# Attention's turned probabilities leave PSUM by two engines instead of one

## The chip, the cores and the metric

One core of one Trainium2 chip. The core has TensorE (PE, matmuls; its weight loads are shown as PEld), VectorE (DVE), ScalarE (ACT), GpSimd (POOL) and SyncE (SP), each with its own program, which it works through in order. They keep step by semaphores. The metric is the device time of one execution in microseconds (us), as the median over runs.

## The reference

Two decoder layers over 512 positions of width 1024: a gated short convolution, then dilated window attention, each followed by a mixture of experts. The change lies in the attention of the second layer: 3 groups of 16 heads with 64 columns each. For one group:

```python
scores = jnp.einsum("bnqrhd,bnkrhd->bnrhqk", qs, kb) * (Dh ** -0.5)
scores = jnp.where(mask[None, :, None, None], scores, -jnp.inf)
m = jnp.max(scores, axis=-1, keepdims=True)
p = jnp.exp(scores - m)
denom = jnp.sum(p, axis=-1)
o = jnp.einsum("bnrhqk,bnkrhd->bnqrhd", p, vb.astype(jnp.float32))
```

Each group's output is divided by its denominator, and the groups are merged with weights from m and denom; then comes the output projection.

## The kernel before

The kernel runs the 16 head slots in two stages (s = 0, 1) of 8. A stage first projects q, k and v for its 8 slots in three groups, then calls `attend(s)`, which every engine has in its own version. `attend` goes through 16 units. A unit u is a pair of heads (head block hb = u // 4, heads hd = 0 and 1) and one tile of 128 queries (t = u % 4). Its keys are up to four tiles of 128: two of the near group and one each of the two far groups, so 512 columns, or 384 where t = 0 and there is no tile before the first.

One unit passes through these steps:

- `scores(u)` on TensorE: q times k into PSUM bank 2*(u%2)+hd. Signal `scored`.
- `mask_scores(u)` on VectorE (L1375): mask, and the row's extreme value, into `prob[u%2]` in SBUF. Four instructions, two per head. Signal `masked`.
- `softmax_exp(u)` on ScalarE (L844): four exponentials in place, with the sums. Signal `expd`.
- `turn_probs(u)` on TensorE (L1764): transposes of the probabilities, head 0 into PSUM bank 4, head 1 into bank 5. Signal `p_turned`, one per head.
- `probs_back(u)` on VectorE (L1387): both banks are copied to `probT[u%2]` in SBUF. Signal `pt_ready`, one per head.
- `weighted(u)` on TensorE (L1778): v times probT into banks 6 and 7. Signal `pv_done`.

The order is written out by hand. In a round u TensorE does scores(u+1), weighted(u-1), turn_probs(u); VectorE mask_scores(u+1), probs_back(u); ScalarE softmax_exp(u+1). At u = 4, 8 and 12 ScalarE also runs `store_heads` (L854, L857), which waits for weighted(u-1) and copies banks 6 and 7 to near_o and far_o; weighted(u) of a new block waits for it (`o_stored`). In stage two ScalarE also has `heads_hi` (L862) at u = 2 and 6, and VectorE `heads_lo` at u = 4 and 8.

Behind the 16 units VectorE does `scales(s)`: 16 small copies (L1394), then a short chain to stat_exp (L1398, signal `gap_in`), which ScalarE takes up (L878), and head_scale (L1404). ScalarE casts a weight block before that (`hi(U_QKV + 7)`). TensorE goes on with matmuls of the next projection (L314 to L316) and, between them, `spread_scales` (L1732), which needs head_scale: in stage one much later, in stage two after 12 matmuls.

Of the kernel before, what the change touches and what calls it, by code (L numbers as in the profile page):

```python
# [31 lines left out]
P = 128  # L32
# [25 lines left out]
def build(nc, x, positions, norm_mix, norm_ffn, norm_final, conv_w_in, conv_w, conv_w_out, attn_w_qkv,  # L58
# [19 lines left out]
    with ExitStack() as ctx:  # L78
# [180 lines left out]
        def sem(name):  # L259
# [26 lines left out]
        scored, masked, expd, p_turned, pt_ready, pv_done, o_stored = (  # L286
            sem("scored"), sem("masked"), sem("expd"), sem("p_turned"), sem("pt_ready"),
            sem("pv_done"), sem("o_stored"))
# [368 lines left out]
        def _(act):  # L657
# [177 lines left out]
            def softmax_exp(u, s):  # L835

                t, buf = u % NT, prob[u % 2]
                for hd in range(2):
                    head = 2 * (u // NT) + hd
                    for far in range(2):  # L840
# [4 lines left out]
                                       scale=-1.0, accum_out=st[:, 1, head:head + 1]).then_inc(expd, 1)  # L845

            def store_heads(hb, s):

                act.wait_ge(pv_done, s * 16 + 4 * hb + 4)
                if s + hb == 0:  # L850
                    act.wait_ge(h_saved, 16 * NT)
                if hb == 0 and s == 1:
                    act.wait_ge(merged, 4)
                act.activation(near_o[s][:, hb, :].rearrange("p (r b a) -> p b r a", r=NT, b=NT),  # L854
                               ps[:, 6, :].rearrange("p (b r a) -> p b r a", r=NT, b=NT), ACT.Copy
                               ).then_inc(o_stored, 1)
                act.activation(far_o[s][:, hb, :], ps[:, 7, :], ACT.Copy).then_inc(o_stored, 1)  # L857
# [7 lines left out]
            def attend(s):  # L865
# [3 lines left out]
                for u in range(16):  # L869
                    if u + 1 < 16:  # L870
                        softmax_exp(u + 1, s)
                    if u % NT == 0 and u:
                        store_heads(u // NT - 1, s)
                    if s == 1 and u in (2, 6):
                        heads_hi(u // 4)
# [50 lines left out]
        def _(dve):  # L926
# [453 lines left out]
            def probs_back(u, s):  # L1380

                if u >= 2:
                    dve.wait_ge(pv_done, s * 16 + u - 1)
                for hd in range(2):
                    dve.wait_ge(p_turned, s * 32 + 2 * u + hd + 1)
                    k0 = P if u % NT == 0 else 0
                    dve.tensor_copy(probT[u % 2][:, hd, k0:S], ps[:, 4 + hd, k0:S]).then_inc(pt_ready, 1)  # L1387

# [91 lines left out]
        def _(pe):  # L1480
# [276 lines left out]
            def turn_probs(u, s):  # L1757

                for hd in range(2):
                    pe.wait_ge(expd, s * 64 + 4 * u + 2 * hd + 2)  # L1760
                    if u >= 1:
                        pe.wait_ge(pt_ready, s * 32 + 2 * (u - 1) + hd + 1)
                    for n in range(1 if u % NT == 0 else 0, 4):
# [4 lines left out]
            def weighted(u, s):  # L1768

                hb, t = u // NT, u % NT  # L1770
                if t == 0 and hb:
                    pe.wait_ge(o_stored, s * 8 + 2 * hb)
                pe.wait_ge(pt_ready, s * 32 + 2 * u + 2)
                keys = ([(0, 0, t - 1)] if t else []) + [(1, 0, t), (2, 1, t), (3, 2, t)]
# [106 lines left out]
```

## Time and profile before

| | |
|---|---|
| Median of 3 runs | 1459.32 us (1459.04 to 1459.7) |
| Profiled execution, its own time | 1458.0 us |
| Its span, first to last instruction | 1456.3 us |
| Busy: TensorE, VectorE, ScalarE | 1363.7, 990.7, 782.9 us |
| Mean granted clock of TensorE | 0.976 |
| Attention, stage one | 737.4 to 789.3 us |
| Attention, stage two | 1003.3 to 1055.2 us |

The profile is of one execution. In a timeline row the first number is the start in us from the span's start and the second the length; one row can hold several instructions (the count stands behind x), and then the length runs from the first start to the last end. Square brackets hold the time the engine sat idle before, and who ended it. An instruction can start before the one ahead of it has ended, so the distance between two starts is often less than the length.

### The profile page before, as it was taken

Reading aid. Unit: us, or ns where it says so; the run is one execution under the profiler, and the core shown is the slowest. Engines: PE = TensorE matmul, PEld = TensorE weight load, DVE = VectorE, ACT = ScalarE, POOL = GpSimd, SP = SyncE. Lnnn points to the kernel's source line nnn. Section 1 sums busy time; section 2 is a strip of 40 time slices with the busy share of each in tenths; the row PEclk is TensorE's granted clock in tenths of the full one; section 3 lists DMA queues with packets and bytes.
Section 4 is the critical chain, followed back from the end, with each engine's and each line's share of the span. In section 5 each row is a group of like instructions: output and inputs, shape, how many; then the busy total and the mean of one; then the engine's idle time right before and its main releaser. Section 6 shows DMA issues by size and latency. Waiting matters only on the chain.

```text
span 1456.3 us, 21039 instructions
## 1 busy us (share of the span) xinstructions
PE 1363.7 (94%) x7335; PEld 1128.7 (78%) x7335; DVE 990.7 (68%) x1289; ACT 782.9 (54%) x947; POOL 209.3 (14%) x309
## 2 busy tenths in 40 slices
PE   4999987999999999999998999999888699999995
PEld 4888776888888877888877888887767588888884
DVE  6455367999999986243466535254846799898998
ACT  4221244888878843523365252335714478888883
POOL 4000021111111212021100202020002111111121
PEclk9999997999999999999999999999999699999998
DMA  6228416999999954232200213221032699999994
GB/s 220 87 95 317 180 72 218 368 391 387 393 391 391 352 226 145 91 111 88 87 31 30 87 59 116 87 87 59 2 116 119 225 368 390 395 379 391 390 356 174
DMA packets 85108, 308.43 MB, mean 212 GB/s; under 512 B 12034, under 2 KB 12058, under 8 KB 68661
## 3 DMA queue, kind: packets, MB, share of 16 engines
q1 hardware_dynamic: 76404, 291.73, 54.0%
q0 software_dynamic: 8640, 15.86, 2.9%
q8 instruction: 39, 0.64, 0.2%
q14 instruction: 25, 0.20, 0.0%
HBM read 291.72 MB, written 31.46 MB: 222 GB/s over the span
## 4 chain that ended last, share of the span: by engine, by line
PE 86%; DVE 7%; issue 2%; ACT 2%; DMA 1%; SPq 1%; POOLq 0%; DVEq 0%; POOL 0%; ACTq 0%
PE ps L314 26%; PE ps L316 25%; PE ps L315 25%; PE ps L1778 2%; PE ps L1591 1%; DVE probT L1387 1%; PE ps L1849 1%; PE ps L1732 1%; PE ps L1764 1%; DVE h L1206 1%; DMA x_rows<-hn_rows,tok_list 1%; ACT prob L844 1%; ACT W_hi L720 1%; PE ps L1606 1%; PE ps L1615 1%
## 5 line engine op out<-in xcount | busy, mean ns | idle before, releaser
L314 PE MATMUL ps<-W_hi,xT_hi_all 128*128 128x512 f32 x1408 | 559.8, 398 | 7.7 <-DVE xT_lo_all L1420 4.5
L316 PE MATMUL ps<-W_hi,xT_lo_all 128*128 128x512 f32 x1408 | 551.8, 392 | 0.0
L315 PE MATMUL ps<-W_lo,xT_hi_all 128*128 128x512 f32 x1408 | 550.4, 391 | 0.0
L1135 DVE TENSOR_TENSOR W_lo<-m_raw,W_hi 128x2048 fp32r<-128x2048 f32 x192 | 435.9, 2291 | 58.7 <-ACT W_hi L720 58.7
L720 ACT ACTIVATE W_hi<-m_raw 128x2048 fp32r<-128x2048 f32 x192 | 367.3, 1915 | 48.2 <-PE ps L316 47.6
L314 PEld LDWEIGHTS ps<-W_hi,xT_hi_all 128*128 128x128 f32 x1408 | 265.7, 189 | 66.1 <-issue 5.0
L316 PEld LDWEIGHTS ps<-W_hi,xT_lo_all 128*128 128x128 f32 x1408 | 265.6, 189 | 57.7
L315 PEld LDWEIGHTS ps<-W_lo,xT_hi_all 128*128 128x128 f32 x1408 | 266.0, 189 | 51.9
L940 DVE SCALAR_TENSOR_TENSOR W_lo<-raw,mix_gain,W_hi 128x512 fp32r<-128x512 f32 x144 | 99.7, 754 | 183.1 <-ACT W_hi L664 183.1
L664 ACT ACTIVATE W_hi<-raw,mix_gain 128x512 fp32r<-128x512 f32 x144 | 92.2, 712 | 228.4 <-issue 224.8
L630 POOL TENSOR_TENSOR qk_rot<-rope_a,rope_b 128x512 f32<-128x512 f32 x48 | 62.3, 1302 | 375.6 <-DVE rope_b L1449 375.6
L946 DVE TENSOR_TENSOR W_lo<-raw,W_hi 128x2048 fp32r<-128x2048 f32 x20 | 45.9, 2293 | 89.1 <-ACT W_hi L668 88.9
L668 ACT ACTIVATE W_hi<-raw 128x2048 fp32r<-128x2048 f32 x20 | 38.2, 1911 | 107.1 <-PE ps L316 104.9
L314 PE MATMUL ps<-xT_hi_all,W_hi 128*128 128x512 f32 x192 | 75.7, 394 | 0.0
L315 PE MATMUL ps<-xT_lo_all,W_hi 128*128 128x512 f32 x192 | 75.2, 392 | 0.0
L316 PE MATMUL ps<-xT_hi_all,W_lo 128*128 128x512 f32 x192 | 75.2, 392 | 0.0
L509 POOL TENSOR_SCALAR msq<-ssq 128x1 f32<-128x1 f32 x20 | 8.9, 444 | 377.7 <-ACT square_out L674 377.6
L737 ACT ACTIVATE xT_hi_all<-ps 128x1024 fp32r<-128x1024 f32 x32 | 32.9, 1027 | 55.8 <-PE ps L1591 55.8
L1446 DVE TENSOR_TENSOR rope_a<-ps,cos_t 128x512 f32<-128x512 f32 x48 | 33.1, 689 | 25.9 <-POOL qk_rot L630 14.1
L1387 DVE COPY probT<-ps 128x512 f32<-128x512 f32 (+1 forms) x64 | 39.1, 653 | 12.4 <-PE ps L1764 11.7
L674 ACT ACTIVATE square_out<-h 128x1024 f32<-128x1024 f32 x20 | 21.1, 1057 | 48.3 <-DVE h L956 30.0
L600 POOL COPY dest_col<-dest_list 128x1 int32 x28 | 18.2, 651 | 181.5 <-ACT y_rows_sb L758 181.5
(232 smaller groups left out, 1458.3 us busy)
## 6 DMA issues: line engine op xcount, KB each, us to landing
m_raw<-in_w_gate_dram SPq DMA_DIRECT2D x64, 1024.0 KB, 7.7
m_raw<-in_w_up_dram SPq DMA_DIRECT2D x64, 1024.0 KB, 8.6
m_raw<-in_w_down_dram SPq DMA_DIRECT2D x64, 1024.0 KB, 8.7
raw<-in_attn_w_qkv_dram SPq DMA_DIRECT2D x36, 1024.0 KB, 5.1
raw<-in_conv_w_in_dram SPq DMA_DIRECT2D x12, 1024.0 KB, 5.1
y_rows<-zero_rows SPq DMA_DIRECT2D x2, 4096.0 KB, 17.4
y_pick<-y_rows SPq DMA_DIRECT2D x16, 512.0 KB, 7.3
raw<-in_conv_w_out_dram SPq DMA_DIRECT2D x4, 1024.0 KB, 5.8
```

Source lines behind the costliest of these rows:

```text
L314: pe.matmul(o, a_hi, b_hi, start=first, stop=False)
L315: pe.matmul(o, a_hi, b_lo, start=False, stop=False)
L316: return pe.matmul(o, a_lo, b_hi, start=False, stop=last)
L630: pool.tensor_tensor(qk_rot[:, r, :], rope_a[r % 2][:, :], rope_b[r % 2][:, :], ALU.add).then_inc(rope_added, 1)
L664: ins = act.activation(W_hi[uc % SPLIT][:, k, :], raw[uc % RAW][:, k, :], ACT.Copy, scale=mix_gain[:, 4 * (uc % 2) + k:4 * (uc % 2) + k + 1])
L668: act.activation(W_hi[uc % SPLIT][:, :, :], raw[uc % RAW][:, :, :], ACT.Copy).then_inc(split_hi, 1)
L720: act.activation(MW_hi[c % MSPLIT][:, :, :], m_raw[c % MRAW][:, :, :], ACT.Copy).then_inc(s["hi"], 1)
L940: ins = dve.scalar_tensor_tensor(out=W_lo[uc % SPLIT][:, k, :], in0=raw[uc % RAW][:, k, :], scalar=mix_gain[:, 4 * (uc % 2) + k:4 * (uc % ...
L946: dve.tensor_tensor(W_lo[uc % SPLIT][:, :, :], raw[uc % RAW][:, :, :], W_hi[uc % SPLIT][:, :, :].bitcast(F), ALU.subtract).then_inc(split_ ...
L1135: dve.tensor_tensor(MW_lo[c % MSPLIT][:, :, :], m_raw[c % MRAW][:, :, :], MW_hi[c % MSPLIT][:, :, :].bitcast(F), ALU.subtract).then_inc(s[ ...
L1387: dve.tensor_copy(probT[u % 2][:, hd, k0:S], ps[:, 4 + hd, k0:S]).then_inc(pt_ready, 1)
L1446: dve.tensor_tensor(av, t, cb, ALU.mult)
```

## The change

In `probs_back` VectorE keeps only the copy of head 0. ScalarE gets a new function `second_back(u, s)`, which copies head 1 from bank 5 with an ACTIVATE Copy of the same size. It stands in ScalarE's round u behind softmax_exp(u+1) and, at u = 4, 8, 12, behind store_heads. The semaphore `pt_ready` becomes two, one for each head; weighted(u) waits for both.

```diff
@@ -284,7 +284,7 @@
         rope_in, rope_added, qk_turned, qkT_ready, v_ready = (
             sem("rope_in"), sem("rope_added"), sem("qk_turned"), sem("qkT_ready"), sem("v_ready"))
         scored, masked, expd, p_turned, pt_ready, pv_done, o_stored = (
-            sem("scored"), sem("masked"), sem("expd"), sem("p_turned"), sem("pt_ready"),
+            sem("scored"), sem("masked"), sem("expd"), sem("p_turned"), [sem("pt_ready0"), sem("pt_ready1")],
             sem("pv_done"), sem("o_stored"))
         gap_in, gap_out, scales_ready, spread, merged = (
             sem("gap_in"), sem("gap_out"), sem("scales_ready"), sem("spread"), sem("merged"))
@@ -844,6 +844,14 @@
                         act.activation(buf[:, hd, cols], buf[:, hd, cols], ACT.Exp, bias=st[:, 0, head:head + 1],
                                        scale=-1.0, accum_out=st[:, 1, head:head + 1]).then_inc(expd, 1)
 
+            def second_back(u, s):
+
+                if u >= 2:
+                    act.wait_ge(pv_done, s * 16 + u - 1)
+                act.wait_ge(p_turned, s * 32 + 2 * u + 2)
+                k0 = P if u % NT == 0 else 0
+                act.activation(probT[u % 2][:, 1, k0:S], ps[:, 5, k0:S], ACT.Copy).then_inc(pt_ready[1], 1)
+
             def store_heads(hb, s):
 
                 act.wait_ge(pv_done, s * 16 + 4 * hb + 4)
@@ -871,6 +879,7 @@
                         softmax_exp(u + 1, s)
                     if u % NT == 0 and u:
                         store_heads(u // NT - 1, s)
+                    second_back(u, s)
                     if s == 1 and u in (2, 6):
                         heads_hi(u // 4)
                 hi(U_QKV + 7, s * 3 + 2)
@@ -1381,10 +1390,9 @@
 
                 if u >= 2:
                     dve.wait_ge(pv_done, s * 16 + u - 1)
-                for hd in range(2):
-                    dve.wait_ge(p_turned, s * 32 + 2 * u + hd + 1)
-                    k0 = P if u % NT == 0 else 0
-                    dve.tensor_copy(probT[u % 2][:, hd, k0:S], ps[:, 4 + hd, k0:S]).then_inc(pt_ready, 1)
+                dve.wait_ge(p_turned, s * 32 + 2 * u + 1)
+                k0 = P if u % NT == 0 else 0
+                dve.tensor_copy(probT[u % 2][:, 0, k0:S], ps[:, 4, k0:S]).then_inc(pt_ready[0], 1)
 
             def scales(s):
 
@@ -1759,7 +1767,7 @@
                 for hd in range(2):
                     pe.wait_ge(expd, s * 64 + 4 * u + 2 * hd + 2)
                     if u >= 1:
-                        pe.wait_ge(pt_ready, s * 32 + 2 * (u - 1) + hd + 1)
+                        pe.wait_ge(pt_ready[hd], s * 16 + u)
                     for n in range(1 if u % NT == 0 else 0, 4):
                         ins = pe.transpose(ps_r[:, 4 + hd, n * P:(n + 1) * P],
                                            prob_r[u % 2][:, hd, n * P:(n + 1) * P], ident_r[:, :])
@@ -1770,7 +1778,8 @@
                 hb, t = u // NT, u % NT
                 if t == 0 and hb:
                     pe.wait_ge(o_stored, s * 8 + 2 * hb)
-                pe.wait_ge(pt_ready, s * 32 + 2 * u + 2)
+                pe.wait_ge(pt_ready[0], s * 16 + u + 1)
+                pe.wait_ge(pt_ready[1], s * 16 + u + 1)
                 keys = ([(0, 0, t - 1)] if t else []) + [(1, 0, t), (2, 1, t), (3, 2, t)]
                 for n, g, kt in keys:
                     for hd in range(2):
```

The program of ScalarE in stage one, from the last exponentials of softmax_exp(5) (buffer prob_101) over the store of the first head block. Before:

```order
L844 ACTIVATE prob_101,near_stat<-prob_101,near_stat 128x256 [waits masked]
L844 ACTIVATE prob_101,stat<-prob_101,stat 128x256 [waits masked]
L844 ACTIVATE prob_101,near_stat<-prob_101,near_stat 128x256 [waits masked]
L844 ACTIVATE prob_101,stat<-prob_101,stat 128x256 [waits masked]
L854 ACTIVATE near_o_106<-ps 128x4x4x32 [waits h_saved,pv_done]
L857 ACTIVATE far_o_108<-ps 128x512
L844 ACTIVATE prob_100,near_stat<-prob_100,near_stat 128x256 [waits masked]
```

After, the same place; probT_104 is the buffer of the even units:

```order
L844 ACTIVATE prob_101,near_stat<-prob_101,near_stat 128x256 [waits masked]
L844 ACTIVATE prob_101,stat<-prob_101,stat 128x256 [waits masked]
L844 ACTIVATE prob_101,near_stat<-prob_101,near_stat 128x256 [waits masked]
L844 ACTIVATE prob_101,stat<-prob_101,stat 128x256 [waits masked]
L862 ACTIVATE near_o_106<-ps 128x4x4x32 [waits h_saved,pv_done]
L865 ACTIVATE far_o_108<-ps 128x512
L853 ACTIVATE probT_104<-ps 128x384 [waits p_turned,pv_done]
L844 ACTIVATE prob_100,near_stat<-prob_100,near_stat 128x256 [waits masked]
```

The copy of u = 4 stands behind exp(5) and the two stores, ahead of exp(6); before, exp(6) followed the stores. In the same way each of the 16 units of a stage has its copy behind the four exponentials of the next unit.

The end of ScalarE's program in stage one, after: the last exponential of u = 15, then the copies of u = 14 and 15, the weight cast, and what answers VectorE's scales.

```order
L844 ACTIVATE prob_101,stat<-prob_101,stat 128x256 [waits masked]
L853 ACTIVATE probT_104<-ps 128x512 [waits p_turned,pv_done]
L853 ACTIVATE probT_105<-ps 128x512 [waits p_turned,pv_done]
L664 ACTIVATE W_hi_53<-raw_58,mix_gain 128x512 [waits mix_gain_in,unit_done,raw_in2]
L664 ACTIVATE W_hi_53<-raw_58,mix_gain 128x512 x3
L887 ACTIVATE stat_exp<-stat_exp 128x64 [waits gap_in]
```

The two copies have come in ahead of the weight cast, which stood right behind the exponentials. On TensorE no matmul moves; the first one of weighted(u) has one wait more. Before, at u = 0:

```order
L1778 MATMUL ps<-probT_104,v_all 64x128 [waits pt_ready]
L1778 MATMUL ps<-probT_104,v_all 64x128 x5
```

After:

```order
L1787 MATMUL ps<-probT_104,v_all 64x128 [waits pt_ready1,pt_ready0]
L1787 MATMUL ps<-probT_104,v_all 64x128 x5
```

The wait on `pt_ready` has become one on `pt_ready1` and one on `pt_ready0`.

## Rows read from the trace of the kernel before

**Rows 1.** The page: its head, and busy time by engine.
```profile
span 1456.3 us, 21039 instructions
...
PE 1363.7 (94%) x7335; PEld 1128.7 (78%) x7335; DVE 990.7 (68%) x1289; ACT 782.9 (54%) x947; POOL 209.3 (14%) x309
```

**Rows 2.** Busy time by stretch, the two attention stages; PEclk is the granted clock.
```profile
737.40:789.30 51.90, 45.30 (x552) 37.88 (x553) 42.40 (x167) 37.28 (x138) 0.00 (x0) 1.00 0.01 2
1003.30:1055.20 51.90, 45.30 (x552) 37.88 (x552) 44.30 (x169) 38.52 (x137) 0.00 (x0) 1.00 0.01 2
```

**Rows 3.** Who waited for whom in stage one: total, times, longest.
```profile
ACT prob L844 <- DVE near_stat L1375: 12.5, 11, 1.6
...
PE ps L1778 <- DVE probT L1387: 2.9, 5, 1.1
...
PE ps L1778 <- ACT far_o L857: 2.2, 3, 0.7
```

**Rows 4.** ScalarE: two source lines (ns min/median/max), two forms in stage one.
```profile
L857 ACT ACTIVATE far_o<-ps x8: 575/577/593, 754.1 to 1058.0; 128x512 f32<-128x512 f32 x8
...
L907 ACT ACTIVATE v_all<-ps,rstd x16: 687/689/698, 660.7 to 1002.6; 128x512 f32<-128x512 f32 x16
...
L844 ACT ACTIVATE prob<-prob,stat 128x256 f32<-128x256 f32 x32 | 15.8, 494 | 0.0
...
L844 ACT ACTIVATE prob<-prob,near_stat 128x128 f32<-128x128 f32 x8 | 3.2, 395 | 3.5 <-DVE near_stat L1375 3.5
```

**Rows 5.** Timeline of stage one, u = 4: start, length, line.
```profile
754.08 0.57 ACT L857 ACTIVATE far_o<-ps 128x512 f32<-128x512 f32 x1
754.55 0.50 ACT L844 ACTIVATE prob<-prob,near_stat 128x256 f32<-128x256 f32 x1
...
754.71 0.88 PE L1778 MATMUL ps<-probT,v_all 128*64 128x128 f32 x12 [0.74 <-ACT far_o L857]
```

**Rows 6.** Timeline of stage one, u = 0.
```profile
742.18 0.49 ACT L844 ACTIVATE prob<-prob,stat 128x256 f32<-128x256 f32 x1
...
742.31 0.88 PE L1778 MATMUL ps<-probT,v_all 128*64 128x128 f32 x12
```

**Rows 7.** Timeline of stage one, u = 2 and 3.
```profile
747.07 0.49 ACT L844 ACTIVATE prob<-prob,stat 128x256 f32<-128x256 f32 x1
...
748.14 1.09 PE L1778 MATMUL ps<-probT,v_all 128*64 128x128 f32 x16 [0.23 <-DVE probT L1387]
749.17 0.87 PE L1764 MATMUL ps<-ident_r,prob_r 128*128 128x128 f32 x8
749.97 0.70 PE L1749 MATMUL ps<-qkT 64*128 64x256 f32 x4
...
751.16 1.09 PE L1778 MATMUL ps<-probT,v_all 128*64 128x128 f32 x16
```

**Rows 8.** Timeline of stage one, the end.
```profile
784.71 2.55 ACT L664 ACTIVATE W_hi<-raw,mix_gain 128x512 fp32r<-128x512 f32 x4
...
786.93 1.29 DVE L1387 COPY probT<-ps 128x512 f32<-128x512 f32 x2 [1.72 <-PE ps L1764]
...
785.26 1.09 PE L1778 MATMUL ps<-probT,v_all 128*64 128x128 f32 x16 [1.11 <-DVE probT L1387]
786.29 0.87 PE L1764 MATMUL ps<-ident_r,prob_r 128*128 128x128 f32 x8
788.28 1.09 PE L1778 MATMUL ps<-probT,v_all 128*64 128x128 f32 x16 [1.11 <-DVE probT L1387]
```

**Rows 9.** Timeline of stage two, heads_hi at u = 2.
```profile
1013.42 1.04 ACT L862 ACTIVATE xT_hi_all<-near_o 128x1024 fp32r<-128x1024 f32 x1
...
1017.02 1.09 PE L1778 MATMUL ps<-probT,v_all 128*64 128x128 f32 x16
```

**Rows 10.** Timeline behind stage two, the first spread matmuls.
```profile
1058.85 1.97 PE L1732 MATMUL ps<-ident,head_scale 128*64 128x128 f32 x32 [0.62 <-DVE head_scale L1404]
```

**Rows 11.** Timeline behind stage one, VectorE's scales.
```profile
791.24 0.23 DVE L1398 TENSOR_TENSOR stat_exp<-stat_min,stat 128x64 f32<-128x64 f32 x1
```

## The prediction

> **What bounds the kernel now.** I read the page first: TensorE is busy for 1363.7 of 1456.3 us [rows 1], so only a stretch where it waits can give anything back. The change touches one piece of code, the attention loop, which runs twice: 737.4 to 789.3 us and 1003.3 to 1055.2 us. The table of these two windows shows the same 51.9 us and the same 45.30 us of TensorE work in both, at full granted clock and with DMA idle [rows 2]. So 6.6 us per stage is all that is on offer, 13.2 us in the two. What follows each stage on TensorE is the projection's matmuls, whose operands are there, so that an end which moves moves everything after it by the same amount.
>
> The waits of the first stage say who ends those 6.6 us [rows 3]. 2.9 us in 5 waits are for VectorE's copy of the turned probabilities (probT, L1387): these the change could touch. 2.2 us in 3 waits are for ScalarE's store of the finished heads (far_o, L857). The remaining 1.5 us lies mostly in the opening, before the first exponentials are done. ScalarE waits 12.5 us for the row minima, so it looks as if it had room for 16 copies. When it has that room is the whole question, since it takes its work in program order.
>
> **The order of one unit.** TensorE does scores(u+1), weighted(u-1), turn(u). ScalarE did softmax_exp(u+1), four exponentials, and at u = 4, 8, 12 then the two copies of store_heads. The new copy for unit u stands behind all of these. weighted(u) needs it, and comes on TensorE right behind scores(u+2). A copy that must queue behind exponentials of the next unit is late; one that finds them done is not. I go through the five kinds of place by rows.
>
> **Price of one copy on ScalarE.** No row of before shows it. The nearest is far_o L857: PSUM to SBUF, 128x512, 577 ns, and the next instruction starts 0.47 to 0.48 us after it [rows 4, 5]. The dear end is L907, the same shape with a per-partition scale, 689 ns; the cheap end is an exponential half as wide, 494 ns [rows 4]. I take 0.58 us, since the new copy, like far_o, has no scale pointer. Going from 128 to 256 columns costs an exponential 0.10 us [rows 4], so the 384-wide copy of a block's first unit is 0.48 us, and its follower starts 0.38 us after it. From the end of a copy to TensorE's start I take 0.05 us: far_o 754.08 + 0.57 = 754.65, matmul 754.71 [rows 5].
>
> **1. Opening, u = 0.** ScalarE has exp(0) and exp(1) back to back, the last at 742.18, 0.49 us long, so the copy starts at 742.67, ends at 743.15, and weighted(0) starts at 743.20. Before it started at 742.31, straight behind the scores [rows 6]. Cost +0.89 us. VectorE's copy of this head had been done by then; on ScalarE it stands behind four exponentials that nobody wants yet.
>
> **2. Turn of a head block, u = 4, 8, 12.** far_o starts at 754.08 and the next instruction at 754.55. That slot now takes the copy: 754.55 + 0.48 + 0.05 = 755.08, against 754.71 [rows 5]. The wait for far_o is followed by one for the copy. Cost +0.37 us, three times: +1.11.
>
> **3. Third unit of a block, u = 2, 6, 10.** The last exponential of exp(3) starts at 747.07, so the copy runs 747.56 to 748.14 and TensorE starts at 748.19; now it starts at 748.14, after a wait of 0.23 for VectorE [rows 7]. One wait takes the place of the other: +0.05, three times, +0.15.
>
> **4. u = 14.** exp(15) holds ScalarE until 784.71; 784.71 + 0.58 + 0.05 = 785.34 against 785.26 [rows 8]. +0.08.
>
> **5. u = 15.** Here ScalarE has nothing before the copy, and the two copies run side by side. turn(15) starts at 786.29, VectorE's first copy at 786.93, 0.64 later, after half the transposes. The other half takes 0.40 more, since eight transposes take 0.80, from 749.17 to the scores at 749.97 [rows 7]. So the copy starts at 787.33 and weighted(15) at 787.96 against 788.28 [rows 8]. -0.32.
>
> The other units cost nothing. At u = 3, turn(3) starts at 749.17, its second half is turned 0.64 + 0.40 later at 750.21, and the four exponentials ahead of the copy are two short and two long ones, done by about then; the copy is in by 750.84, and weighted(3) started at 751.16 [rows 7]. So it has 0.3 us in hand, and u = 5 has as much, where TensorE and ScalarE have both been set back by the block's turn. In the second stage heads_hi (L862, 1.04 us) stands behind the copy at u = 2 and 6. From 1013.42 on: copy 0.48, heads 0.95, four exponentials 1.76, then the copy of u = 3 with 0.63 ends at 1017.24, while weighted(3) started at 1017.02 [rows 9]. These 0.22 us are hidden: scores(5) is already issued, so exp(5) and the store behind it come when they came, and weighted(4) waits longer than that in any case.
>
> **Sum.** Stage one: 0.89 + 1.11 + 0.15 + 0.08 - 0.32 = +1.91. Stage two has the same terms, but its end hangs on VectorE: the spread matmuls wait 0.62 us for head_scale [rows 10], whose chain starts as soon as VectorE's copies end. With one copy fewer it starts 1.29 - 0.69 = 0.60 earlier, and TensorE's own path 0.32 earlier with 0.62 of slack, so the end term is -0.60: +1.63. Together +3.54 us. ScalarE's part of the head_scale chain stays covered: it must be free when VectorE hands over, 791.24 + 0.23 - 0.60 = 790.9, and after the copy (787.33 + 0.48) and the four weight casts (2.55) it is free at 790.4 [rows 8, 11]. If that cover failed, the cost would be some tenths in stage two only. The weight casts themselves start 3 us later, but VectorE's half of that split stands behind head_scale in its program, so no DMA is released later for it; DMA is idle in both stages [rows 2]. The two semaphores instead of one add a second wait to weighted(u); o_stored beside pt_ready was already such a pair at u = 4, and nothing there shows a price. VectorE's saved time, 16 x 0.6 us a stage, buys nothing while its masks start on scores.
>
> The profiled execution took 1458.0 us, so it would be 1461.5. The median of the runs shown is 1459.32, 1.3 above it, and the times are compared with that: 1459.32 + 3.54 = **1462.9 us**, 0.24% slower. About 0.2% (2.9 us) is what a measurement of this kernel can tell from no change, so this stands close to that line.
>
> **Bounds.** Nine of the copies in a stage lie on the path in this account (1 + 3 + 3 + 1 + 1). With 0.49 us a copy it is 9 x 0.09 = 0.8 less in each stage, total +1.9. With 0.69 it is 9 x 0.11 = 1.0 more in each, total +5.5.
>
> **Rivals.**
> - **Faster: the copies run side by side everywhere.** For it: ScalarE's 12.5 us of waiting and VectorE with both copies in a row [rows 3, 8]. Then the three waits of 0.23 vanish and both closing waits shrink by 0.32, the opening and far_o stay as they are: -1.3 in stage one, -1.6 in stage two, 1456.4 us. It decides if ScalarE reaches the copy before TensorE has turned the second head. Against it: at 742.67, 747.56, 754.55 and 784.71 ScalarE comes free only after that, and its idle time lies ahead of the exponentials, not behind them. The Trainium skill speaks for this rival: "Perfetto Trace Analysis", section Optimizing Scalar/DVE Operations, says that where VectorE is saturated, handing work to ScalarE may make sense, and "TensorEngine Tiling (Array Packing)", section PSUM Bottleneck, says to use both engines to empty PSUM. By that rule the copies' waits would fall; this trace agrees only at u = 15, and there by 0.32 us. Chance 6%.
> - **No change that can be measured: the copy is nearer the cheap end**, or a place hides some tenths. TensorE would start weighted(4) at 754.99 instead of 755.08, and so on; +1.9, 1461.2 us. Against it: far_o is the same operation on the same engine. Chance 28%.
> - **Slower by more: the copy is as dear as L907**, or waiting for the fresh transposes costs ScalarE more than it cost VectorE: +5.5, 1464.8 us. Against it: L907 has the scale pointer. Chance 10%.
>
> My forecast has 56%, with its own range from 1462.2 to 1464. Slower by over 0.2% is forecast plus the dear copy, 66%; within 0.2% is 28%; faster by over 0.2% is 6%. For the 8 in 10 I go from 1460.4, a little under the cheap copy, to 1465.1, over the dear one; the faster rival stays outside.
>
> **What would show it.** In the profile after: 32 ScalarE copies of about 580 ns and 480 ns; no idle time of ScalarE ahead of those at u = 0, 2, 4, 14; TensorE's waits before the weighted matmuls naming ScalarE's probT, about 1.1 us at u = 4, 8, 12 in place of 0.74, about 0.9 at u = 0, 0.28 at u = 2, 0.8 at u = 15; each stage 53.8 us. The wait for head_scale after stage two is near 0.3 us. It is wrong if weighted(4) starts no later behind far_o, if weighted(0) follows the scores at once, or if a copy lasts outside 0.49 to 0.69 us. It is also wrong if a later stretch, the projection or the experts, changes its length by more than 0.5 us.

## The result and the profile after

The changed kernel took 1463.22 us (median of 8 runs, 1460.83 to 1464.43), the kernel before beside it 1459.26 us (8 runs, 1458.24 to 1460.8). The ratio, run against run, is 1.0024 with a 95% interval of 1.0013 to 1.0035, which is 1.9 to 5.1 us: slower, and by no more than what can just be told. The forecast was 1462.9 us. A second comparison, further down, gave 1.0031 [1.0019, 1.0042].

The page after, for [rows 1], its head and busy time by engine:

```profile
span 1460.2 us, 21093 instructions
...
PE 1361.8 (93%) x7335; PEld 1128.4 (77%) x7335; DVE 973.1 (67%) x1257; ACT 798.1 (55%) x979; POOL 209.0 (14%) x309
```

VectorE has lost 17.6 us of work and 32 instructions, ScalarE has gained 15.2 us and 32, and the span is 3.9 us longer. Taking work off VectorE has bought nothing. The windows of the two stages, for [rows 2] (a window here is longer because the stages are):

```profile
737.70:792.30 54.60, 44.90 (x553) 38.15 (x553) 34.06 (x153) 43.89 (x153) 0.00 (x0) 1.00 0.01 2
1006.30:1060.90 54.60, 45.07 (x553) 38.23 (x553) 36.19 (x155) 45.36 (x153) 0.00 (x0) 1.00 0.01 2
```

TensorE does the same work at the same granted clock, over a longer time: the loss is waiting. Who waits for whom in stage one, for [rows 3] (total us, times, longest):

```profile
DVE prob L1384 <- PE ps L1760: 17.6, 15, 8.8
...
PE ps L1787 <- ACT probT L853: 8.6, 9, 1.4
ACT prob L844 <- DVE near_stat L1384: 7.8, 8, 1.6
```

The five waits for VectorE's probT and the three for far_o (2.9 and 2.2 us) are gone. Nine waits for ScalarE's probT stand in their place, 8.6 us. Exactly the nine places of the prediction: u = 0, 2, 4, 6, 8, 10, 12, 14 and 15. ScalarE's waiting for VectorE's minima fell from 12.5 to 7.8 us, so it did have room, but the room lay ahead of its exponentials. VectorE's saved time turned into waiting: 7.8 us more for scores in this stage (17.6 for 9.8) and 3.5 us more for transposes (10.0 for 6.5).

To see where the time goes I use three marks that every kernel has: stage one and stage two, each from its first score matmul to the start of weighted(15), and for stage two also the first matmul of the spread.

| profile | stage one | stage two | stage two to spread | spread to end of span |
|---|---|---|---|---|
| before | 50.80 | 50.83 | 55.50 | 397.4 |
| changed | 53.53 | 53.49 | 57.84 | 396.1 |
| changed, run again | 53.52 | 53.53 | 57.87 | 396.5 |
| before, run again | 50.81 | 50.83 | 55.50 | 397.2 |

In these two pairs a stage repeats to 0.05 us. The rest of the span does not: the code behind the spread is the same in all kernels here and took 395.9 to 397.4 us in 13 profiles, and stage one started anywhere from 737.2 to 739.8 us. Between the two stages all show 215.1 us. So the change costs 2.73 us in stage one and 2.34 us up to the spread, 5.07 us, where the prediction had 1.91 and 1.63. In the first pair of profiles the unchanged code behind the spread gave 1.4 us of it back. Where it did so can be read from the granted clock, here over 14 us from 16 us behind the first spread matmul on, before and then after:

```profile
1074.80:1088.80 14.00, 9.47 (x41) 7.45 (x36) 5.50 (x5) 2.86 (x2) 0.00 (x0) 0.76 0.56 195
1080.20:1094.20 14.00, 9.47 (x43) 7.57 (x38) 5.49 (x5) 2.86 (x2) 0.00 (x0) 0.88 0.54 200
```

TensorE had the lower of its two clocks (1.2 and 2.4 GHz) for a larger part of this stretch before (0.76) than after (0.88), and at its end the kernel before was 0.9 of the 1.4 us behind. All 13 profiles fall into two groups by the clock of this stretch: seven with 0.76 took 396.9 to 397.4 us behind the spread, six with 0.88 took 395.9 to 396.7.

The timeline after. The opening, for [rows 6] (start, length, engine, line; in brackets the wait and whom for):

```profile
742.43 0.49 ACT L844 ACTIVATE prob<-prob,stat 128x256 f32<-128x256 f32 x1
...
742.92 0.47 ACT L853 ACTIVATE probT<-ps 128x384 f32<-128x384 f32 x1
...
743.53 0.88 PE L1787 MATMUL ps<-probT,v_all 128*64 128x128 f32 x12 [0.91 <-ACT probT L853]
```

The copy starts when the last exponential of the next unit is through, with no idle time ahead of it. At u = 2 and 3, for [rows 7]:

```profile
748.78 0.57 ACT L853 ACTIVATE probT<-ps 128x512 f32<-128x512 f32 x1
...
749.50 1.09 PE L1787 MATMUL ps<-probT,v_all 128*64 128x128 f32 x16 [0.50 <-ACT probT L853]
...
751.33 0.70 PE L1757 MATMUL ps<-qkT 64*128 64x256 f32 x4
...
752.40 1.09 PE L1787 MATMUL ps<-probT,v_all 128*64 128x128 f32 x16
```

At u = 4, for [rows 5]; the copy has taken the slot behind far_o:

```profile
755.43 0.58 ACT L865 ACTIVATE far_o<-ps 128x512 f32<-128x512 f32 x1
755.91 0.47 ACT L853 ACTIVATE probT<-ps 128x384 f32<-128x384 f32 x1
...
756.53 0.88 PE L1787 MATMUL ps<-probT,v_all 128*64 128x128 f32 x12 [1.32 <-ACT probT L853]
```

The end, for [rows 8]:

```profile
787.79 0.57 ACT L853 ACTIVATE probT<-ps 128x512 f32<-128x512 f32 x1
790.51 0.60 ACT L853 ACTIVATE probT<-ps 128x512 f32<-128x512 f32 x1 [2.15 <-PE ps L1772]
...
788.51 1.09 PE L1787 MATMUL ps<-probT,v_all 128*64 128x128 f32 x16 [1.36 <-ACT probT L853]
...
791.25 1.09 PE L1787 MATMUL ps<-probT,v_all 128*64 128x128 f32 x16 [0.84 <-ACT probT L853]
```

Only at u = 15 does ScalarE wait for the transposes rather than TensorE for ScalarE's queue, and only there is the wait shorter than before (0.84 against 1.11). One number returns in every row: from the end of the copy to the matmul it is not 0.05 us. 742.92 + 0.47 = 743.39, and TensorE starts at 743.53; 755.91 + 0.47 = 756.38 and 756.53; 787.79 + 0.57 = 788.36 and 788.51. It is 0.14 to 0.15 us each time.

### The profile page after: what moved, and what is told of

Read it like the earlier page. It is cut to its first block, busy times and chain, and to the rows that moved or that the text cites. A ratio compares the mean times of both kernels' runs of the same rounds, so it can differ in the third digit from the quotient of the medians.

```text
span 1460.2 us, 21093 instructions
## 1 busy us (share of the span) xinstructions
PE 1361.8 (93%) x7335; PEld 1128.4 (77%) x7335; DVE 973.1 (67%) x1257; ACT 798.1 (55%) x979; POOL 209.0 (14%) x309
## 4 chain that ended last, share of the span: by engine, by line
PE 85%; DVE 5%; ACT 5%; issue 2%; DMA 1%; SPq 1%; POOLq 0%; DVEq 0%; ACTq 0%; POOL 0%
PE ps L314 26%; PE ps L316 25%; PE ps L315 25%; ACT prob L844 2%; PE ps L1599 1%; PE ps L1787 1%; PE ps L1858 1%; PE ps L1740 1%; PE ps L1772 1%; DVE h L1215 1%; DMA x_rows<-hn_rows,tok_list 1%; ACT W_hi L720 1%; PE ps L1757 1%; PE ps L1614 1%; PE ps L1502 1%
## 5 line engine op out<-in xcount | busy, mean ns | idle before, releaser
L1787 PE MATMUL ps<-probT,v_all 128*64 128x128 f32 x480 | 33.3, 278 | 17.0 <-ACT probT L853 17.0
L1384 DVE CUSTOM_DVE_ANT_0 prob<-ps,near_mask 128x256 f32<-128x256 f32 (+1 forms) x64 | 24.8, 388 | 34.9 <-PE ps L1760 34.9
```

The source lines that it names most:

```text
L1787: ins = pe.matmul(ps[HD * hd:HD * hd + HD, 6 if g == 0 else 7, t * P:(t + 1) * P], v_all[:, g, kt, head * HD:head * HD + HD], probT[u % 2] ...
```

## Experiments

Two questions. Is it the place in ScalarE's program that costs, or what the copies cost anywhere? And whose are the 0.09 us that each release is longer: ScalarE's as the engine that copies, or the second semaphore's? Differences of time are against the kernel before run on the same chip.

**One semaphore** (changed kernel, both copies increment one counter):

```
-  ...ps[:, 5, k0:S], ACT.Copy).then_inc(pt_ready[1], 1)      # ScalarE; VectorE alike
+  ...ps[:, 5, k0:S], ACT.Copy).then_inc(pt_ready, 1)
-  pe.wait_ge(pt_ready[0], s * 16 + u + 1)
-  pe.wait_ge(pt_ready[1], s * 16 + u + 1)
+  pe.wait_ge(pt_ready, s * 32 + 2 * u + 2)
   ...in turn_probs, which now waits for both copies and not for its head's alone
-  pe.wait_ge(pt_ready[hd], s * 16 + u)
+  pe.wait_ge(pt_ready, s * 32 + 2 * u)
```

> The changed kernel with one semaphore pt_ready again, which both engines raise; ScalarE still copies the second head. Measured so far from the first score matmul to the start of weighted(15): before 50.80 and 50.83 us in the two stages, changed 53.53 and 53.49. In the changed trace TensorE starts 0.15 us after the end of ScalarE's copy (copy of u = 14 787.79 + 0.57 = 788.36, matmul 788.51), where I had taken 0.05. Theory A (the second wait on weighted costs 0.10 us each time the copy is what it waits for): nine such places a stage, 0.9 us less, stages near 52.6 us, and the gap from copy to matmul back at 0.05 to 0.06. Theory B (the gap belongs to ScalarE's copy, whatever the semaphores): stages stay at 53.5 and the gap at 0.15. Both leave the time over the kernel before, by 3.5 us (A: near 2).

1463.75 against 1459.42 us, 1.003 [1.002, 1.004]; stages 52.97 and 52.95, 0.56 and 0.54 shorter than the changed kernel's. At u = 14:

```profile
788.85 0.58 ACT L853 ACTIVATE probT<-ps 128x512 f32<-128x512 f32 x1
...
789.48 1.09 PE L1786 MATMUL ps<-probT,v_all 128*64 128x128 f32 x16 [1.28 <-ACT probT L853]
```

788.85 + 0.58 = 789.43, and the matmul starts 0.05 later, as far_o's did in [rows 5]. So ScalarE as the releaser is not what makes it long. The copies keep a cost of 2.17 us in stage one with one semaphore. But not all nine places gained. At u = 4 the matmul waits for o_stored first and for the one semaphore second, and it is the second that fires last:

```profile
757.17 0.48 ACT L853 ACTIVATE probT<-ps 128x384 f32<-128x384 f32 x1
...
757.79 0.88 PE L1786 MATMUL ps<-probT,v_all 128*64 128x128 f32 x12 [1.31 <-ACT probT L853]
```

757.17 + 0.48 = 757.65, and 0.14 to the matmul, as with two semaphores; u = 8 and 12 are the same. Six places with 0.09 less are 0.54 us, and 0.56 was measured.

**Two semaphores, both copies on VectorE** (kernel before, only the semaphores changed):

```
-  dve.tensor_copy(probT[u % 2][:, hd, k0:S], ps[:, 4 + hd, k0:S]).then_inc(pt_ready, 1)
+  dve.tensor_copy(probT[u % 2][:, hd, k0:S], ps[:, 4 + hd, k0:S]).then_inc(pt_ready[hd], 1)
-  pe.wait_ge(pt_ready, s * 32 + 2 * u + 2)
+  pe.wait_ge(pt_ready[0], s * 16 + u + 1)
+  pe.wait_ge(pt_ready[1], s * 16 + u + 1)
   ...in turn_probs
-  pe.wait_ge(pt_ready, s * 32 + 2 * (u - 1) + hd + 1)
+  pe.wait_ge(pt_ready[hd], s * 16 + u)
```

> The kernel before with pt_ready split into one semaphore for each head; both copies stay on VectorE. The other part of the change alone. Theory A (second wait costs 0.10): TensorE starts 0.15 us after VectorE's copy ends instead of 0.05, and since it waits for that copy in most units but the block firsts, each stage grows by 0.7 to 0.9 us, to 51.5 to 51.7, +1.5 us in all, too little for the timing to tell. Theory B (it is ScalarE's copy): stages stay at 50.8 and the gap at 0.05.

1460.11 against 1459.42, 1.0002 [0.9993, 1.0011]: the timing shows no difference, and its upper end is 1.6 us; the marks show one, 0.87 us in stage one and 0.93 up to the spread. Stages 51.67 and 51.84, +0.87 and +1.01, with not one copy moved. At u = 14:

```profile
786.85 1.29 DVE L1387 COPY probT<-ps 128x512 f32<-128x512 f32 x2 [0.30 <-PE ps L1764]
...
788.28 1.09 PE L1779 MATMUL ps<-probT,v_all 128*64 128x128 f32 x16 [1.20 <-DVE probT L1387]
```

786.85 + 1.29 = 788.14, and 0.14 to the matmul. In the kernel before the pair of copies of u = 15, 786.93 + 1.29 = 788.22, released its matmul at 788.28 [rows 8], after 0.06; the other units there show 0.05 to 0.06, and the ones here 0.14 to 0.15. So 0.08 to 0.09 us comes with the second wait, whichever engine copies. The waits named for the copies grew by just that, 1.11 to 1.20 and 0.23 to 0.33. The waits for far_o at u = 4, 8 and 12 fell, from 0.74 to 0.66: they take up what the unit ahead of them lost.

**The order of the two waits swapped** (changed kernel):

```
-  pe.wait_ge(pt_ready[0], s * 16 + u + 1)
   pe.wait_ge(pt_ready[1], s * 16 + u + 1)
+  pe.wait_ge(pt_ready[0], s * 16 + u + 1)
```

> The changed kernel with the two waits of weighted written the other way round: first the one that ScalarE's copy ends (pt_ready[1]), then VectorE's (pt_ready[0]), which has long been raised. Before, at u = 4, 8, 12, weighted also had two waits, o_stored first and pt_ready second; far_o's o_stored came last and TensorE started 0.05 us behind it. In the changed kernel and with two semaphores on VectorE the wait that fires last is the second in the program, and the gap is 0.14 to 0.15. Theory D (the price depends on which of the waits fires last: none when it is the first): gap back at 0.05, waits 0.82, 0.41, about 1.22, 1.27, 0.75, stages near 52.7 us. Theory E (a second wait costs 0.09 wherever it stands): nothing changes, 0.91, 0.50, 1.32, 1.36, 0.84 and 53.5 us.

1464.04 against 1458.86, 1.0035 [1.0021, 1.0049] (five runs; a sixth took 3468 us and is left out); stages 52.84 and 52.81, 0.69 and 0.68 shorter by the marks, which the timing doesn't resolve. At u = 14:

```profile
786.75 0.58 ACT L853 ACTIVATE probT<-ps 128x512 f32<-128x512 f32 x1
...
787.38 1.09 PE L1787 MATMUL ps<-probT,v_all 128*64 128x128 f32 x16 [1.28 <-ACT probT L853]
```

787.33 to 787.38, 0.05 again, with both semaphores and both waits in place. So it isn't the number of waits but the order: when the wait that is first in the program fires last, the matmul follows after 0.05 us; when the second fires last, after 0.14. At u = 4 there are three waits, on o_stored, on ScalarE's copy and on VectorE's, and the middle one fires last:

```profile
755.20 0.47 ACT L853 ACTIVATE probT<-ps 128x384 f32<-128x384 f32 x1
...
755.77 0.88 PE L1787 MATMUL ps<-probT,v_all 128*64 128x128 f32 x12 [1.27 <-ACT far_o L865]
```

755.20 + 0.47 = 755.67, and 0.10 to the matmul; the view names far_o, but far_o ended 0.47 us before it. Six places with 0.09 less and three with 0.05 less are 0.69 us, which is what stage one lost. The order also says why [rows 5] misled: there the first wait in the program, on o_stored, was the one that fired last. The same pair fired the other way round in the kernel with one semaphore, and showed 0.14. Why the later wait costs more, no run here shows.

**Everything between the two heads** (changed kernel; the stores and the copy come after the next unit's first head, ahead of its second; the same instructions in another order):

```
-  softmax_exp(u + 1, s)
+  softmax_exp(u + 1, s, (0,))
   ...store_heads(u // NT - 1, s) where a block turns
   second_back(u, s)
+  if u + 1 < 16:
+      softmax_exp(u + 1, s, (1,))
```

> The changed kernel with ScalarE's program in another order: exponentials of head 0 of unit u+1, then at u = 4, 8, 12 the two stores, then the copy of unit u, then the exponentials of head 1. Same work, same semaphores. Theory A (the copy is late because it stands behind four exponentials and the stores): the copy finds its transposes just done; the waits of weighted fall from 0.91 to about 0.1 at u = 0, from 0.50 to 0.1 at u = 2, 6, 10, from 1.32 to 0.4 at u = 4, 8, 12 and from 1.36 to 0.9 at u = 14. Sum 0.8 + 1.2 + 2.8 + 0.4 = 5.2 us less a stage, some of it lost again in stage two where heads_hi stands in between: stages near 48 and 49 us, 1453 to 1455 us, below the kernel before by about 5. Theory C (32 more copies on ScalarE are too much work for it wherever they stand, or reading PSUM from two engines at once slows both): the stages stay over 51 us and the time over 1459.

1452.19 against 1459.42, 0.9956 [0.9942, 0.9969]: 0.44% faster, stages 47.51 and 48.30. Each copy starts two exponentials earlier. At u = 4 in stage one:

```profile
753.15 0.58 ACT L865 ACTIVATE far_o<-ps 128x512 f32<-128x512 f32 x1
753.63 0.48 ACT L853 ACTIVATE probT<-ps 128x384 f32<-128x384 f32 x1
754.00 0.51 ACT L844 ACTIVATE prob<-prob,near_stat 128x256 f32<-128x256 f32 x1
...
754.25 0.88 PE L1789 MATMUL ps<-probT,v_all 128*64 128x128 f32 x12 [0.33 <-ACT probT L853]
```

The copies, their price, both semaphores and their order are those of the changed kernel. Only the place of the copies and of the stores is new, and 6.0 us of stage one has gone (53.53 to 47.51). The loss is one of place; the next two runs tell the copies' place from the stores'. Two engines that read PSUM side by side do not slow each other here: VectorE's longest copy took 692 ns in the changed kernel and 693 before.

**Stores between the heads, no copy moved** (kernel before, the same split of softmax_exp around store_heads alone):

```
-  softmax_exp(u + 1, s)
+  softmax_exp(u + 1, s, (0,))
   ...store_heads(u // NT - 1, s) where a block turns
+  if u + 1 < 16:
+      softmax_exp(u + 1, s, (1,))
```

> The kernel before (both copies on VectorE, one semaphore), with one thing in ScalarE's order: store_heads stands between the exponentials of the two heads of unit u+1 and not behind them. It separates how much of the gain of the reordered kernel (stages 47.51 and 48.30 us) comes from the stores alone. By rows of before: far_o would end 0.98 us earlier (two exponentials of 0.49), which takes the whole wait of 0.74 away at u = 4, 8, 12: 2.2 us less in stage one, near 48.4, and a little less in stage two, where heads_lo on VectorE now has its 1.1 us in the way: 48.5 to 50. Time near 1456. If TensorE only meets another wait there, the exponentials of head 1 for turn(5), the stages stay over 50 us.

1455.45 against 1458.98, 0.9977 [0.9967, 0.9986]; stages 48.43 and 50.05. The wait for far_o at a block's turn, 0.74 us in [rows 5], is gone. In stage two a new one has come, at u = 5 and 9, because VectorE does heads_lo (1.22 us) ahead of the two copies:

```profile
1018.52 1.22 DVE L1422 TENSOR_TENSOR xT_lo_all<-near_o,xT_hi_all 128x1024 fp32r<-128x1024 f32 x1
...
1022.37 0.88 PE L1780 MATMUL ps<-probT,v_all 128*64 128x128 f32 x12 [0.85 <-DVE probT L1389]
```

Against the kernel before, the stores' place alone gives 2.4 us in stage one and 0.8 in stage two; with the copies moved as well it was 3.3 and 2.5. So a little over half of the gain, by the marks, needs no copy on ScalarE. The rest does: 0.9 us in stage one, and 1.75 in stage two, where the new wait for VectorE stood.

**Copy between the heads, stores behind both** (changed kernel, second_back moved alone):

```
-  softmax_exp(u + 1, s)
+  softmax_exp(u + 1, s, (0,))
+  second_back(u, s)
+  if u + 1 < 16:
+      softmax_exp(u + 1, s, (1,))
   ...store_heads(u // NT - 1, s) where a block turns
-  second_back(u, s)
```

> The changed kernel with the copy between the exponentials of the two heads, but the stores left behind them. With the reordered kernel (47.5 and 48.3) and the changed one (53.5 and 53.5) this splits the gain. u = 0 loses its wait of 0.91, u = 2, 6, 10 theirs of 0.50, u = 14 half a microsecond: 0.9 + 1.5 + 0.5 = 2.9 less; at u = 4, 8, 12 far_o still ends behind four exponentials and now a copy, so there 1.3 us of wait stay, with far_o named instead of probT. Stages 50.6 to 51.4 us, second stage up to 52; near 1459 us, no difference to before that can be told. If copies alone were the problem and the stores not, the stages would be at 48.5 already.

1460.11 against 1458.98, 1.0006 [0.9995, 1.0017]; stages 52.41 and 51.75. Stage one looks too long for the expectation, but 1.4 us of it is TensorE's clock in this one execution. The same 32 matmul instructions, from weighted(4) to weighted(5) and from weighted(8) to weighted(9):

```profile
756.77:759.47 2.70, 2.70 (x32) 2.29 (x33) 0.69 (x1) 1.83 (x7) 0.00 (x0) 1.00 0.00 0
769.43:773.54 4.11, 4.11 (x32) 3.43 (x32) 0.69 (x1) 2.24 (x8) 0.00 (x0) 0.58 0.00 0
```

The granted clock was 0.58 in the second, so for most of it the lower of the two, and it took 1.41 us longer. No other attention stage of the 13 profiles shows this. At full clock stage one is about 51.0 us (an estimate, 52.41 less 1.41), inside the expectation: 0.2 over the kernel before and 2.5 below the changed kernel, with the stores at the same place in all three. u = 0 and 2 no longer wait, but the block's turn is worse than in the changed kernel:

```profile
754.28 0.49 ACT L853 ACTIVATE probT<-ps 128x384 f32<-128x384 f32 x1 [0.17 <-PE ps L1774]
...
756.77 0.88 PE L1789 MATMUL ps<-probT,v_all 128*64 128x128 f32 x12 [1.51 <-ACT far_o L865]
```

The copy waits 0.17 us for the second head's transposes, and behind it stand two exponentials and both stores, which weighted(4) needs. The edit moves one late link and pushes another back.

**Copies of the odd units only** (ScalarE copies at odd u, VectorE does both heads at even u; two semaphores):

```
-  second_back(u, s)
+  if u % 2 == 1:
+      second_back(u, s)
-  ...one copy of head 0 on VectorE
+  for hd in range(1 if u % 2 == 1 else 2): ...
```

> ScalarE copies the second head at odd u alone; at even u VectorE copies both as before. Two semaphores. This leaves out all places where I found a loss (u = 0, 2, 4, 6, 8, 10, 12, 14) and keeps u = 15. By the account of places: u = 15 still gains 0.3, the waits at u = 2, 6, 10 are for VectorE again; with the second wait at 0.10 at about six places it is even: stages at 50.5 to 51.7 us against 50.8, no change in time that can be told. If instead the loss is spread over all copies in proportion to their number, half of it stays: stages near 52.2 us, 1461.3 us. The wait at u = 2 also tells theory A from B: both copies are VectorE's there and there are two semaphores; gap 0.15 by A, 0.05 by B.

1459.39 against 1459.42, 0.9998 [0.9988, 1.0007]; stages 51.05 and 51.99. u = 15 keeps its gain (0.84), and u = 14 shows 1.20 for the second semaphore. far_o shows 0.85, where two semaphores alone gave 0.66: the odd unit ahead, with its copy on ScalarE, takes 2.90 us instead of 3.01 before, and the block's turn gives that back. New are 0.50 at u = 1 and 0.40 at u = 5 and 9 of stage two. In the changed kernel the odd units are free, as I read it, because u = 0 and each turn of a block have set TensorE back first; here nothing has at u = 1 (its weighted(0) doesn't wait), and the copy is late. That rests on the order of the rows alone.

**Copies of a block's first unit only**, u = 0, 4, 8, 12, the same edit with u % NT == 0:

```
-  second_back(u, s)
+  if u % NT == 0:
+      second_back(u, s)
-  ...one copy of head 0 on VectorE
+  for hd in range(1 if u % NT == 0 else 2): ...
```

> ScalarE copies the second head only in the first unit of each block (u = 0, 4, 8, 12), in the place of the changed kernel, behind the exponentials and the stores; elsewhere VectorE copies both. Two semaphores. 4 copies a stage moved instead of 16. By the account of places this keeps the two largest terms: a wait of 0.9 us at u = 0 and about 1.2 us for probT in place of 0.74 for far_o at u = 4, 8, 12, and adds 0.09 at each of VectorE's releases (u = 2, 6, 10, 14, 15 had 0.33, 0.33, 0.33, 1.20, 1.20 with two semaphores). Stages 53.3 to 53.9 us against 50.8 before and 53.5 with all 16 copies moved, 1462 to 1464 us. If the loss went with the number of copies moved, a quarter of it would show: stages near 51.5 us, 1460.5 us.

1465.08 against 1458.98, 1.004 [1.0025, 1.0056]; stages 53.94 and 53.90. The second semaphore is in it too (0.87 by itself), as in the changed kernel, and the gain at u = 15 isn't. Four copies moved cost as much as all sixteen:

```profile
745.54 0.88 PE L1789 MATMUL ps<-probT,v_all 128*64 128x128 f32 x12 [0.91 <-ACT probT L853]
...
751.47 1.09 PE L1789 MATMUL ps<-probT,v_all 128*64 128x128 f32 x16 [0.33 <-DVE probT L1397]
...
758.51 0.88 PE L1789 MATMUL ps<-probT,v_all 128*64 128x128 f32 x12 [1.12 <-ACT probT L853]
```

What the loop pays goes by where the copies stand, not by how many there are.

**The parts that were good, together** (kernel before; stores and copies between the heads, one semaphore, VectorE keeps both copies of a block's first unit):

```
-  softmax_exp(u + 1, s)
+  softmax_exp(u + 1, s, (0,))
   ...store_heads(u // NT - 1, s) where a block turns
+  if u % NT:
+      second_back(u, s)
+  if u + 1 < 16:
+      softmax_exp(u + 1, s, (1,))
   ...VectorE
-  for hd in range(2):
+  for hd in range(1 if u % NT else 2):
   ...in turn_probs
-  pe.wait_ge(pt_ready, s * 32 + 2 * (u - 1) + hd + 1)
+  pe.wait_ge(pt_ready, s * 32 + 2 * u)
```

> What the runs point to, together: the stores and the copy between the exponentials of the two heads; ScalarE copies head 1 except in a block's first unit, where VectorE copies both (0.33 us of wait for probT was left there); one semaphore, which saves 0.09 us at each copy that is waited for. Against the reordered kernel (47.51 and 48.30 us) it should lose the waits of 0.34 at u = 4, 8, 12 and 0.09 in each of u = 14 and 15, and part of the 0.3 at u = 3 and 7 of stage two: stages 45.9 to 46.5 and 47.2 to 48.0 us, 1450 to 1451 us, 0.6% below the kernel before. If taking the copy off ScalarE puts VectorE's second copy in the way, which ends 0.6 us later, nothing is won: 1452.

1450.93 us (1449.09 to 1451.59) against 1458.98, 0.994 [0.9926, 0.9953]: 0.6% faster, the fastest kernel of the study. Stages 45.96 and 47.26. In stage one the weighted matmuls wait at two places only:

```profile
783.14 1.09 PE L1790 MATMUL ps<-probT,v_all 128*64 128x128 f32 x16 [0.75 <-ACT probT L853]
785.79 1.09 PE L1790 MATMUL ps<-probT,v_all 128*64 128x128 f32 x16 [0.75 <-ACT probT L853]
```

**Both kernels once more**, unedited, the changed one timed in 7 runs, the one before profiled once:

> The changed kernel once more, unchanged, for another profile of it. In its first profile the two stages took 5.1 us more than before, up to the spread matmuls, but the whole only 3.9, because what follows took 396.04 us against 397.45, code that the change does not touch. In the nine other profiles that part took 395.9 to 397.4 us. If it is scatter from one execution to the next, it takes another value here, in that band, while the stages stay at 53.5 and 57.8. If the change shortens it, it is again at 396.0.

> The kernel before once more, for a second profile: stages 50.8 us and 55.5 to the spread matmuls again; the part behind them somewhere in 395.9 to 397.5 us if it is scatter, 397.4 if it belongs to this kernel.

1464.02 against 1458.86 us, 1.0031 [1.0019, 1.0042]. The marks came back within 0.04 us (table above), and the code behind the spread gave 396.5 and 397.2 us. So what the marks show is the kernel's. The difference behind the spread is not fixed, 1.4 us in the first pair and 0.75 in the second, but it kept its sign, and the granted clock of the stretch shown with the first pair was again 0.88 for the changed kernel and 0.76 for the one before. The copies on ScalarE are not what makes it: with one semaphore and with the waits swapped the same 16 copies a stage went with 0.76, 397.1 and 397.2 us.

## Why the prediction was right, and which term was off

The sign, the mechanism and the nine places came out as worked; 1463.22 was measured for 1462.9. The sum was 1.5 us too low in the profile, 5.07 for 3.54. The timings, +3.96 (1.9 to 5.1) and 1.0031, hold either. The close total is partly luck: the span grew by 3.9 us only because the code behind the spread had the better clock. The 5.07 of the marks is nearer to the +5.5 of the dear rival, though not by its reason.

- **Price of the copy: right.** The profile gives 32 copies of 467 to 597 ns, median 575, for 0.58 us taken, and 0.48 for the 384-wide ones.

```profile
L853 ACT ACTIVATE probT<-ps x32: 467/575/597, 742.9 to 1059.1; 128x512 f32<-128x512 f32 x24, 128x384 f32<-128x384 f32 x8
```

- **Release of 0.05 us, in the price of a copy: the mis-sized term.** It measured 0.14 to 0.15 at all nine places, 9 x 0.09 = 0.8 us a stage; 1.91 + 0.8 = 2.7, and 2.73 was measured. "The two semaphores instead of one add a second wait to weighted(u); o_stored beside pt_ready was already such a pair at u = 4, and nothing there shows a price" is the sentence that failed. The pair had its late wait in first place. The swapped order and the one semaphore both bring 0.05 back at the six places without o_stored, where the late wait is then first or alone; at the other three they leave 0.10 and 0.14. Two semaphores alone add 0.87 to the kernel before. One wait in [rows 8] and the first of two in [rows 5] were no bound for the second of two. I should have kept a term for it.
- **The steps, place by place.** I take the start of each weighted matmul from the start of its stage, after less before. u = 0: 5.81 less 4.83 = +0.98, forecast +0.89 and the release 0.09. u = 2 and the odd unit ahead of it: +0.14, forecast +0.05 and 0.09; u = 4 and the odd unit ahead: +0.46, forecast +0.37 and 0.09; u = 14 with u = 13: +0.17, forecast +0.08 and 0.09. u = 15: -0.28, forecast -0.32, so here 0.05 of the 0.09 was made good. 0.98 + 3 x 0.14 + 3 x 0.46 + 0.17 - 0.28 = 2.67; u = 6 and 10 gave 0.16 instead of 0.14, and the rest to 2.73 is rounding.
- **The odd units' 0: right only together with the even ones.** From its scores to weighted(3) it took 1.19 us before (749.97 to 751.16, [rows 7]) and takes 1.07 now (751.33 to 752.40), with no wait named in either. Before, it started 0.06 after VectorE's pair of copies, so these were what held it, by less than the view names:

```profile
749.81 1.29 DVE L1387 COPY probT<-ps 128x512 f32<-128x512 f32 x2 [0.62 <-PE ps L1764]
```

Each odd unit gains 0.09 to 0.12 so, and the next even one gives it back, since its masks start with its scores and its exponentials stay as late as they were. That is why the even units' waits grew by more than the stage did: by 0.27 at u = 2, where two places together cost 0.14, and by 0.58 at u = 4, where they cost 0.46. It is also why the waits came out at 0.50 and 1.32, where the signs had 0.28 and about 1.1.
- **heads_hi at u = 2 and 6 of stage two: right**, 0.22 hidden. weighted(3) waits 0.20, and weighted(4) 1.04 instead of the 1.32 of stage one:

```profile
1021.26 1.09 PE L1787 MATMUL ps<-probT,v_all 128*64 128x128 f32 x16 [0.20 <-ACT probT L853]
...
1025.12 0.88 PE L1787 MATMUL ps<-probT,v_all 128*64 128x128 f32 x12 [1.04 <-ACT probT L853]
```

- **The end of stage two: right.** The wait for head_scale was to fall from 0.62 [rows 10] to about 0.3, and the stage to give back 0.28 more than stage one; it gave 0.39 (2.73 less 2.34). The release explains the difference: at u = 15 of stage two nothing on the way to head_scale waits for weighted(15), so only eight of the nine places count there, and 1.63 + 8 x 0.09 = 2.35 (an estimate) for 2.34 measured:

```profile
1064.16 1.97 PE L1740 MATMUL ps<-ident,head_scale 128*64 128x128 f32 x32 [0.30 <-DVE head_scale L1412]
```

- **"Wrong if a later stretch changes its length by more than 0.5 us":** it did, by 1.4 and then by 0.75, and this was a bad test. The same kernel moves there by 0.2 (before) and 0.4 us (changed) from one profile to the next, over 13 profiles with the same code it scattered by 1.5, and it goes with the granted clock of the stretch shown above.

Of the rivals, the dear copy is out by its duration, and the cheap one too. The faster rival was wrong for this order of the program, for the reason given, that ScalarE's idle time lies ahead of the exponentials. Part of it was right for another one: with stores and copies between the heads the time is 0.44% below the kernel before, where the stores between the heads alone gave 0.23%, so the split is worth about half of it there. The Trainium skill's advice to empty PSUM with both engines ("TensorEngine Tiling (Array Packing)", section PSUM Bottleneck) is thus neither borne out nor refuted by one number: +0.24% with the copies behind the exponentials, 1.0006 with the copies alone between them, and -0.44% with copies and stores between them.

What stays open: what decides how long the clock is low behind the spread, and whether a kernel's program has a part in it; and why the timing shows no difference between the changed kernel and the swapped one (1.0031 and 1.0035, where the marks say 1.4 us less). The two intervals overlap over far more than 1.4 us, which is 0.1%.

## What to carry to other kernels

An engine's share of idle time doesn't say whether a piece of work fits on it; ask what stands ahead of the new instruction in its program, and when the idle time comes. Split the work and choose the place together: here the copies cost 0.24% behind four exponentials, and nothing that the timing can tell once they stood between them. With the stores there too the whole gave 0.44%, of which the stores alone give about half, and with four copies a stage left to VectorE and one semaphore 0.6%. Where an instruction waits for two semaphores, put the one that fires last first.

## What the runs showed that I had not expected

- With two waits on a matmul, the start comes 0.14 to 0.15 us after the last release when the wait that fires last is the second in the program, and 0.05 us when it is the first, or the only one. With three waits and the middle one last it is 0.10. ScalarE and VectorE as releasers give the same.
- Delays that the profile doesn't name as a wait held about 0.1 us each, seven times a stage; they show only as a longer step from scores to weighted (1.19 us against 1.07).
- A stretch of 397 us with the same instructions scatters by 1.5 us between profiles, and goes with how long TensorE had its lower clock in it (0.76 or 0.88 in the same 14 us), while the attention stages of 50 us repeat to 0.05 at full clock. One stage in 26 had a granted clock of 0.58 over 4 us and was 1.4 us longer. For an effect of 0.2% the marks of one stage tell more than the span or the timing, if the granted clock in it is looked at too.
